# Two query units multiplied side by side, value pages and key stores placed earlier, and work regrouped at three joins of a decoder layer

## The chip, the cores and the metric

The kernel runs on one NeuronCore of one Trainium2 chip. The metric is the time of one execution on the device in microseconds (us). TensorE (PE) multiplies, VectorE (DVE) and ScalarE (ACT) work elementwise, GpSimd (POOL) does a little elementwise work and issues transfers, and SyncE (SP) issues most transfers. Sixteen DMA engines move the data.

## What is computed

One layer of a decoder in fp32 for 256 prompt tokens and 8 sampled tokens (T = 264 columns): a mixer with eight gated delta-net heads and eight block-attention heads, cross attention, and a gated feed-forward, each followed by a layer norm of residual plus result.

```python
def gated_delta_chunked(q, k, v, beta, g): ...   # 8 heads, chunks of 64
def moba_attend(q, kb, vb, kmean, q_pos, rel_bias):
    gate = jnp.einsum('bqhd,bhnd->bqhn', qf, kmean)
    top_s, top_i = lax.top_k(gate, K)            # 3 blocks of 256 cached tokens per sample and head
    kg = kb[bi, hi, idx]; vg = vb[bi, hi, idx]
    ...
    p = jax.nn.softmax(s.reshape(B, Q, H, -1), axis=-1).reshape(s.shape)
    return jnp.einsum('bqhtk,bqhtkd->bqhd', p, vg)

def post_norm(x, sub, g, b):
    return layer_norm(ALPHA * x + sub, g, b)
...
xp = post_norm(xp, mix_p, ln_g[l, 0], ln_b[l, 0])
xp = post_norm(xp, cross_attend(xp, mkp, mvp, x_wq[l], x_wo[l]), ln_g[l, 1], ln_b[l, 1])
xp = post_norm(xp, swiglu(xp, ffn_w1[l], ffn_w2[l]), ln_g[l, 2], ln_b[l, 2])
```

## The kernel before

The work is a sequence of *units*. A unit is one weight tile of 2048 inputs by 128 outputs (1 MB in fp32). Its product with the 264 columns keeps fp32 precision by a split: ACT rounds the tile to its upper part `wh` (L498, `upper`), DVE makes the rest `wl` (L503, `lower`), and PE adds three products for each of the 16 slices of the contraction, `wh*xh` (L519), `wh*xl` (L520) and `wl*xh` (L521), 48 matmuls in all, into one of two banks of `psum_g`. `raw`, `wh` and `wl` have two slots, used in turn by even and odd units. SP loads a tile with `load_unit` (L493) once its slot has been read (`raw_used`). Counting semaphores tie the stages: `raw_full`, `hi_done`, `raw_used`, `mm_done`, `psum_free`. All orders are written out by hand, engine by engine.

The stages, in units: `q` (8, the queries of block attention), `a` (32, the projections of the delta-net heads and the keys of block attention, with 128 pages of cached keys scored in between, L2122), `b` (16, units 32 to 47 of a joint count `u`: eight value units, then eight gates "z"), `out` (16), `wk`, `xq`, `wv`, `xo` (4 each, cross attention), and the feed-forward.

*Start.* SP loads the input x in quarters, each followed by a quarter of unit 0's tile (L615, L616), then unit 1, then 1.1 MB of constants and tables, then unit 2. ACT and DVE split x and the quarters (L865, L867, L1299, L1302). PE multiplies unit 0, then the small products for the gates (`ab`, L2073), then unit 1, a product that turns them (`abt`, L2089 to L2091), units 2, 3 and 4, and the products of the running sums (`cum`, L2097 to L2100). Between the copies of units 2 and 3 ACT computes a sigmoid and a logarithm, with two table loads (L885, L887), and only behind them the upper part of unit 4.

*Value pages.* For each sample and head six pages of cached values (64 KB each, 512 bytes per row) are needed, chosen at run time. They come in 16 groups of four heads. Two heads of a group are loaded by SP and two by GpSimd (`values`, L596 for the page numbers, L604 for twelve loads each). There is room for three groups: group g waits until group g - 3 was used. PE uses a group in 24 products (`page_values`, L2254). `groups_at(u, end)` says which: group 0 after unit 35, group 1 in the middle of unit 36, group 2 behind it, and so on, so that group 15 is used in the middle of unit 43.

GpSimd's own list there is: store a state, clear `zp` (L798), the decay product `tg` of head pair 3 (`decays(3)`, L775), which PE reads in unit 35, the value pages, the store of the last state (L785), and later the store of all keys and values `kv` (L817). SP's list behind its last value group is: four sample states (L671), unit 45, the other four states once GpSimd's last state store has landed (`s_out`), unit 46, rows of the result to a scratch (L706), unit 47.

*Join to the output product.* ACT and DVE split four groups of the mixer's result in the order 2, 3, 0, 1 (L1074, L1102 and L1707); ahead of group 0 DVE gates the last head and the samples (L1577, L1704). ACT then loads a table (L1136) and makes the upper part of unit 1 of `out`.

*Layer norms.* DVE centres and scales groups of `xf` (L1744, L1750), ACT applies gain and offset (L1124) and, in the first norm, the upper part (L1131), DVE the lower (L1758). The first norm has groups of 2, 2, 4, 4 and 4 slices, the last one of 4, 4, 4, 2 and 2. The first norm runs beside the four `wk` units; PE needs its last group for the last quarter of unit 0 of `xq`, and unit 1 of `xq` is split by ACT and DVE behind that group.

## Time and profile before

| what | value |
| --- | --- |
| median of 3 executions | 1602.91 us (1602.39 to 1605.07) |
| the profiled execution's own time | 1602.35 us |
| its span, first to last instruction | 1600.4 us |
| PE busy | 1540.7 us (96%) |
| DVE, ACT, POOL busy | 932.9, 644.2, 182.7 us |
| moved | 365.17 MB, mean 228 GB/s |

The profiled execution is 0.56 us below the median, and 1.95 us of it lie outside its span. PE is busy nearly all the time, so a time is won only where PE stands still or runs at the lower clock, and the profile has to be read at those places.

### The profile page before, as it was taken

The numbers are of one execution on the slowest core, as the hardware profiler recorded it, in microseconds if no ns is written. First come the engines' busy times: TensorE is split into PE (matmuls) and PEld (weight loads), VectorE is DVE, ScalarE is ACT, GpSimd is POOL, SyncE is SP. The second block draws the span as 40 slices with busy tenths as digits, with TensorE's granted clock in tenths as the row PEclk, the third lists the DMA queues.
The fourth block names the chain that finished last, engine by engine and source line by source line (L and its number), as shares of the span: only waits on it lengthen the run. The fifth ranks groups of instructions, "written<-read, shape, count | busy, mean of one in ns | idle before, by whom it ended". The sixth has DMA issues, their size and how long they took to land.

```text
span 1600.4 us, 36185 instructions
## 1 busy us (share of the span) xinstructions
PE 1540.7 (96%) x14680; PEld 1495.3 (93%) x14680; DVE 932.9 (58%) x1130; ACT 644.2 (40%) x752; POOL 182.7 (11%) x286
## 2 busy tenths in 40 slices
PE   7999999999998879999999999999999999999996
PEld 6999999999898779997899999999999999999995
DVE  4445645557753345774487666666666644445566
ACT  5344333343523443464454333544333333333344
POOL 0000202021577510001000000000011000000000
PEclk9999999999999999999999999999999999999998
DMA  8698878886788977455645545555677655555453
GB/s 308 218 338 338 314 282 331 290 319 219 222 250 259 288 281 309 172 184 200 244 163 183 172 171 183 185 180 187 241 261 255 214 185 183 184 183 174 165 179 113
DMA packets 104339, 365.17 MB, mean 228 GB/s; under 512 B 14385, under 2 KB 48378, under 8 KB 77210
## 3 DMA queue, kind: packets, MB, share of 16 engines
q1 hardware_dynamic: 89682, 322.66, 58.0%
q0 software_dynamic: 12752, 39.73, 7.2%
q10 hardware_dynamic: 1792, 1.20, 0.4%
q8 instruction: 79, 1.29, 0.3%
q14 instruction: 34, 0.28, 0.1%
HBM read 353.27 MB, written 10.47 MB: 227 GB/s over the span
## 4 chain that ended last, share of the span: by engine, by line
PE 76%; issue 8%; ACT 5%; DVE 5%; DMA 4%; SPq 2%; POOLq 1%; POOL 1%; ACTq 0%; DVEq 0%
PE psum_g L519 21%; PE psum_g L520 21%; PE psum_g L521 21%; PE M L2122 3%; PE M L2137 3%; DVE wl L503 2%; ACT wh L498 2%; DMA raw<-w_in_t 1%; PE M L519 1%; PE psum_g L2431 1%; PE M L520 1%; PE M L521 1%; DMA sraw<-cache_k_t 1%; SPq L630 1%; ACT xf L1124 1%
## 5 line engine op out<-in xcount | busy, mean ns | idle before, releaser
L519 PE MATMUL psum_g<-xh,wh 128*128 128x264 f32 (+1 forms) x2414 | 709.0, 294 | 24.0 <-DVE wl L503 11.9
L520 PE MATMUL psum_g<-xl,wh 128*128 128x264 f32 (+1 forms) x2414 | 688.8, 285 | 0.0
L521 PE MATMUL psum_g<-xh,wl 128*128 128x264 f32 (+1 forms) x2414 | 687.9, 285 | 0.0
L503 DVE TENSOR_TENSOR wl<-raw,wh 128x2048 fp32r<-128x2048 f32 (+1 forms) x223 | 502.6, 2254 | 310.6 <-ACT wh L498 310.1
L498 ACT CAST wh<-raw 128x2048 fp32r<-128x2048 f32 (+1 forms) x223 | 418.2, 1875 | 248.9 <-PE psum_g L521 204.4
L519 PEld LDWEIGHTS psum_g<-xh,wh 128*128 128x128 f32 x2414 | 458.6, 190 | 40.3 <-issue 23.1
L520 PEld LDWEIGHTS psum_g<-xl,wh 128*128 128x128 f32 x2414 | 458.8, 190 | 3.1 <-issue 2.9
L521 PEld LDWEIGHTS psum_g<-xh,wl 128*128 128x128 f32 x2414 | 457.0, 189 | 0.0
L519 PE MATMUL psum_g<-gh,wh 128*128 128x264 f32 x704 | 200.4, 285 | 0.2 <-DVE wl L503 0.2
L521 PE MATMUL psum_g<-gh,wl 128*128 128x264 f32 x704 | 199.4, 283 | 0.0
L520 PE MATMUL psum_g<-gl,wh 128*128 128x264 f32 x704 | 199.4, 283 | 0.0
L519 PEld LDWEIGHTS psum_g<-gh,wh 128*128 128x128 f32 x704 | 132.5, 188 | 0.6 <-DVE wl L503 0.4
L520 PEld LDWEIGHTS psum_g<-gl,wh 128*128 128x128 f32 x704 | 132.7, 188 | 0.0
L521 PEld LDWEIGHTS psum_g<-gh,wl 128*128 128x128 f32 x704 | 132.0, 187 | 0.0
L2122 PE MATMUL M<-kring,pj 128*32 128x128 f32 x1536 | 61.9, 274 | 0.9 <-DMA sraw<-cache_k_t 0.9
L2137 PE MATMUL M<-chain 128*128 128x128 f32 x448 | 60.4, 276 | 0.1
L2122 PEld LDWEIGHTS M<-kring,pj 128*32 128x32 f32 x1536 | 53.9, 110 | 6.5 <-issue 4.2
L847 POOL DMA_DIRECT2D out_dn_sample<-state x8 | 7.2, 904 | 445.8 <-DVE state L2019 445.8
L604 POOL DMA_DIRECT2D pj<-cache_v x102 | 55.0, 539 | 14.7 <-issue 9.8
L2137 PEld LDWEIGHTS M<-chain 128*128 128x128 f32 x448 | 55.0, 191 | 1.6 <-issue 1.2
L1260 ACT ACTIVATE sg<-psum_g 128x264 f32<-128x264 f32 x28 | 11.0, 392 | 111.1 <-PE psum_g L521 111.1
L1110 ACT ACTIVATE xt<-xf 128x264 f32<-128x264 f32 x32 | 13.6, 425 | 99.8 <-DVE xf L1803 56.0
(431 smaller groups left out, 1698.6 us busy)
## 6 DMA issues: line engine op xcount, KB each, us to landing
raw<-w_t SPq DMA_DIRECT2D x88, 1024.0 KB, 4.9
raw<-w_in_t SPq DMA_DIRECT2D x55, 1024.0 KB, 7.8
kring<-cache_k_t SPq DMA_DIRECT2D x96, 512.0 KB, 4.6
sraw<-cache_k_t SPq DMA_DIRECT2D x32, 512.0 KB, 6.1
raw<-w_out_t SPq DMA_DIRECT2D x16, 1024.0 KB, 5.1
raw<-w2a_t SPq DMA_DIRECT2D x16, 1024.0 KB, 4.8
raw<-w2b_t SPq DMA_DIRECT2D x16, 1024.0 KB, 4.9
raw<-w2c_t SPq DMA_DIRECT2D x16, 768.0 KB, 4.2
```

The costliest lines, as they stand in the source:

```text
L498: nc.scalar.copy(wh[:, u % 2, 0:nk], raw[:, u % 2, 0:nk]).then_inc(hi_done, 1)
L503: eng.tensor_tensor(wl[:, u % 2, 0:nk], raw[:, u % 2, 0:nk], wh[:, u % 2, 0:nk].bitcast(F32), ALU.subtract).then_inc(raw_used, 1)
L519: nc.tensor.matmul(out, hi_w, x_hi(k), start=(k == order[0]), stop=False)
L520: nc.tensor.matmul(out, hi_w, x_lo(k), start=False, stop=False)
L521: last = nc.tensor.matmul(out, lo_w, x_hi(k), start=False, stop=(k == order[-1]))
L604: eng.dma_start(v_pages[s][:, t], a["cache_v"][0, ds(pages[6 * n_ + t], 1), :, h].rearrange("a t d -> t (a d)"))\
L630: _, pages = nc.values_load_multi_w_load_instructions(page_turns[j:j + 1], engines={mybir.EngineType.SP}, min_val=0, max_val=k_pages.shape ...
L1110: nc.scalar.activation(xt[:, u % 2], m, ACT.Square).then_inc(sq_made, 1)
L1124: ins = nc.scalar.activation(xf[:, k], xf[:, k], ACT.Identity, bias=ln_gb[:, 1, i, k:k + 1], scale=ln_gb[:, 0, i, k:k + 1])
L2122: last = nc.tensor.matmul(M[rows:rows + 32, pg // 4, (pg % 4) * P:(pg % 4 + 1) * P], qz[:, b + 4 * (p % 2), h], k_slot(m)[:, h * P:(h + 1) ...
L2137: last = nc.tensor.matmul(out(w), lhs(w), rhs(w), start=True, stop=True)
L2431: last = nc.tensor.matmul(psum_g[:, t], m[:, 4 * u + k, t * P:(t + 1) * P], w_at(w, k), start=(u == 0 and k == 0 and w is wh and m is mem_ ...
```

## The change

The diff, cut to its core:

```diff
         def groups_at(u, end):
 
-            group = 2 * (u - KEY_UNITS - 3) + end - 1
-            return (group,) if 0 <= group < 16 else ()
+            first = 2 * (u - KEY_UNITS - 3)
+            groups = {(0, 1): (0,), (2, 0): (1,), (2, 1): (2, 3)}.get((first, end), (first + end,) if first > 2 else ())
+            return tuple(g for g in groups if g < 16)
...
-        E_OUT = 16 * 2
+        E_OUT = 16 * 3
...
+            parts = [slice(per * g, per * (g + 1)) for g in range(PARTS)]
+            first, second, third = (w_tile(a["w_in_t"], KTAIL + u) for u in range(3))
+            for g, part in enumerate(parts):
+                end = g == PARTS - 1
                 sp.dma_start(x_in[:, part], a["x_t"][:, part]).then_inc(d_x[g], 16)
-                sp.dma_start(raw[:, 0, part], w_tile(a["w_in_t"], KTAIL)[:, part])\
-                  .then_inc(d_w[g] if g < PARTS - 1 else raw_full[0], 16)
-            load_unit(sp, turn, 1, w_tile(a["w_in_t"], KTAIL + 1))
-            sp.dma_start(C[:], a["constants"]).then_inc(d_const, 16)
+                sp.dma_start(raw[:, 0, part], first[:, part]).then_inc(raw_full[0] if end else d_w[g], 16)
+                sp.dma_start(raw[:, 1, part], second[:, part]).then_inc(raw_full[1] if end else d_v[g], 16)
+            for g, part in enumerate(parts):
+                wait(sp, s_dve, f"lw{g}")
+                sp.dma_start(raw[:, 0, part], third[:, part]).then_inc(raw_full[0] if g == PARTS - 1 else d_y[g], 16)
+            sp.dma_start(C[:, 0:P], a["constants"][:, 0:P]).then_inc(d_eye, 16)
+            load_unit(sp, turn, 3, w_tile(a["w_in_t"], KTAIL + 3))
+            sp.dma_start(C[:, P:], a["constants"][:, P:]).then_inc(d_const, 16)
...
-            for u in range(2, 4 * n):
+            for u in range(4, 4 * n):
                 load_unit(sp, turn + u // 4, u % 4, w_tile(a["w_in_t"], KTAIL + u))
-                if 3 <= u < 7:
-                    half = u - 3
-                    load_pages(half // 2, range(2 * (half % 2), 2 * (half % 2) + 2))
+                half = u - 4
+                load_pages(half // 2, range(2 * (half % 2), 2 * (half % 2) + 2))
...
             nc.gpsimd.memset(zp_flat, 0.0).then_inc(e_pool.sem, 1)
-            decays(3)
+            pool.wait_ge(psum_free, 4 * turn + KEY_UNITS + 2)
+            pool.dma_start(o["kv"][:, 0:8], kv[:, 0:8]).then_inc(e_out, 16)
             pool.wait_ge(pid_back, 16)
             values(0)
+            decays(3)
             values(1)
...
-            for name, tile in (("kv", kv), ("edge", edge)):
-                pool.dma_start(o[name], tile[:]).then_inc(e_out, 16)
+            pool.dma_start(o["kv"][:, 8:16], kv[:, 8:16]).then_inc(e_out, 16)
+            pool.dma_start(o["edge"], edge[:]).then_inc(e_out, 16)
...
+                act.wait_ge(d_v[g] if g < PARTS - 1 else raw_full[1], 16)
+                nc.scalar.copy(wh[:, 1, part], raw[:, 1, part]).then_inc(s_act.sem, 1)
+            act.sem_inc(hi_done, 2)
...
-
-            upper_next(act, turn, 0)
+                scaled(u)
+
             unit_done(act, turn, 0)
-            nc.scalar.mul(qb[:, 0], psum_g[:, 0, 0:T], SCALE).then_inc(psum_free, 1)
+            for g in range(2):
+                act.wait_ge(d_y[g], 16)
+            nc.scalar.copy(wh[:, 0, 0:2 * per], raw[:, 0, 0:2 * per]).then_inc(s_act.sem, 1)
+            act.wait_ge(d_y[2], 16)
+            act.wait_ge(raw_full[0], 32)
+            nc.scalar.copy(wh[:, 0, 2 * per:], raw[:, 0, 2 * per:]).then_inc(hi_done, 1)
+            scaled(0)
+            scaled(1)
             wait(act, s_pe, "ab")
             nc.scalar.copy(abt, M[:, 0, 0:T]).then_inc(s_act.sem, 1)
-            queries(1)
             queries(2)
+            upper_next(act, turn, 3)
...
-            queries(3)
+            scaled(3)
...
-            act.preload_act_table_set("natural_log_exp_and_others")
             for i in range(n):
                 for u in range(4):
                     upper_next(act, turn + i, u)
+                    if i == 0 and u == 0:
+                        act.preload_act_table_set("natural_log_exp_and_others")
...
                        after={1: lambda: (memory_keys(1), upper_next(act, turn, 2)),
-                              2: lambda: (memory_keys(2), upper_next(act, turn, 3))})
-            memory_keys(3)
+                              2: lambda: (memory_keys(2), upper_next(act, turn, 3)),
+                              3: lambda: (memory_keys(3), upper_next(act, STAGES["xq"][0], 0))})
             turn, n = STAGES["xq"]
             for u in range(4):
-                upper_next(act, turn, u)
+                if u:
+                    upper_next(act, turn, u)
...
+                wait(dve, s_act, f"hv{g}")
+                nc.vector.tensor_tensor(wl[:, 1, part], raw[:, 1, part], wh[:, 1, part].bitcast(F32),
+                                        ALU.subtract).then_inc(s_dve.sem, 1)
+            wait(dve, s_dve, f"lv{PARTS - 1}")
+            dve.sem_inc(raw_used, 2)
             turn, n = STAGES["q"]
-            lower_next(dve, turn, 0)
-            settle(dve)
+            wait(dve, s_act, "h2")
+            nc.vector.tensor_tensor(wl[:, 0, 0:2 * per], raw[:, 0, 0:2 * per], wh[:, 0, 0:2 * per].bitcast(F32),
+                                    ALU.subtract).then_inc(s_dve.sem, 1)
+            dve.wait_ge(hi_done, 3)
+            nc.vector.tensor_tensor(wl[:, 0, 2 * per:], raw[:, 0, 2 * per:], wh[:, 0, 2 * per:].bitcast(F32),
+                                    ALU.subtract).then_inc(raw_used, 1)
+            dve.wait_ge(d_eye, 16)
...
-                if g == 0:
+                if g == 3:
                     gated(H - 1)
...
+                    for g in (4, 5):
                         centre(g)
                         scale(g)
-                    low(2)
-                low(3)
-                low(4)
+                    low(3)
+                    at("n5")
+                    low(4)
+                    low(5)
...
-            def quarter(k):
-                if k % per == 0:
-                    wait(pe, s_dve, f"lw{k // per}")
-
-            products(pe, psum_g[:, 0, 0:T], 0, lambda w, s, k: w[:, s, k], XH, XL, KC, before=quarter, done=mm_done)
+            for g in range(PARTS):
+                for s in range(2):
+                    wait(pe, s_dve, f"l{'wv'[s]}{g}")
+                    for k in range(per * g, per * (g + 1)):
+                        out, end = psum_g[:, s, 0:T], k == KC - 1
+                        nc.tensor.matmul(out, wh[:, s, k], xh[:, k], start=(k == 0), stop=False)
+                        nc.tensor.matmul(out, wh[:, s, k], xl[:, k], start=False, stop=False)
+                        last = nc.tensor.matmul(out, wl[:, s, k], xh[:, k], start=False, stop=end)
+                        if end:
+                            last.then_inc(mm_done, 1)
             pe.wait_ge(d_ab, 16)
             for i in range(4):
                 last = ab_products(i)
             last.then_inc(s_pe.sem, 1)
-            unit(pe, turn, 1, XH, XL)
+            wait(pe, s_dve, "l2")
+            pe.wait_ge(psum_free, 3)
+            products(pe, psum_g[:, 0, 0:T], 0, lambda w, s, k: w[:, s, k], XH, XL, KC,
+                     before=lambda k: pe.wait_ge(raw_used, 5) if k == 2 * per else None, done=mm_done)
...
-            unit(pe, turn, 2, XH, XL)
```

- **Start.** Units 0 and 1 are loaded, split and multiplied quarter by quarter side by side; unit 2's tile is loaded in quarters as the quarters of unit 0 become free; the constants come as a small first part (the identity, with a semaphore of its own) and a rest behind unit 3. PE runs the `ab` product behind both units and `abt` behind unit 2. The upper part of unit 4 stands ahead of ACT's table loads.
- **Value pages.** GpSimd issues its part of group 0 ahead of `decays(3)`. Groups 2 and 3 are both used behind unit 36, and each later group half a unit before its former place, so that group 15 is used behind unit 42. `kv` is stored in two halves: the keys ahead of GpSimd's value pages once unit 31 has been copied, the values at the old place (`E_OUT` counts three transfers).
- **Join to the output product.** DVE does the last gate and the samples between groups 2 and 3, and ACT loads its table behind the upper part of unit 1.
- **Layer norms.** Both norms now have groups of 2, 2, 4, 4, 2 and 2 slices; in the first, the split of unit 1 of `xq` stands ahead of the last two groups' lower parts (`n5`), on ACT ahead of the last two groups.

On ACT near the start, before (the cast `wh<-raw` of 128x2048 is a whole unit's upper part, `qb<-psum_g` the copy of a finished unit; row 28 is the upper part of unit 4):

```order
18 L498 CAST wh<-raw 128x2048
19 L875 ACTIVATE qb<-psum_g 128x264
20 L498 CAST wh<-raw 128x2048
21 L875 ACTIVATE qb<-psum_g 128x264
22 L885 ACT_TABLE_LOAD
23 L885 ACTIVATE sigm<-kv 128x24
24 L887 ACT_TABLE_LOAD
25 L888 ACTIVATE kv<-kv 128x24
26 L890 ACTIVATE kv<-kv 128x24
27 L892 ACTIVATE kv<-kv 128x8
28 L498 CAST wh<-raw 128x2048
29 L875 ACTIVATE qb<-psum_g 128x264
```

And in the changed program:

```order
22 L898 COPY kv<-M 128x264
23 L497 CAST wh<-raw 128x2048
24 L882 ACTIVATE qb<-psum_g 128x264
25 L497 CAST wh<-raw 128x2048
26 L902 ACT_TABLE_LOAD
27 L902 ACTIVATE sigm<-kv 128x24
28 L904 ACT_TABLE_LOAD
29 L905 ACTIVATE kv<-kv 128x24
30 L907 ACTIVATE kv<-kv 128x24
31 L909 ACTIVATE kv<-kv 128x8
32 L882 ACTIVATE qb<-psum_g 128x264
```

The upper part of unit 4 (row 25) now stands ahead of both table loads.

On POOL behind the state store of pair 2, before (`chain<-C,g_hc` is `decays(3)`; the loads from `cache_v` go on to the twelfth):

```order
26 L785 DMA out_dn_prompt<-chain 128x2x128
27 L798 MEMSET kring 128x720
28 L775 TENSOR_TENSOR chain<-C,g_hc 128x512
29 L596 TENSOR_LOAD C
30 L604 ISA
31 L604 DMA pj<-cache_v 128x128
32 L604 ISA
```

And in the changed program, with the place where group 0 ends shown too:

```order
26 L789 DMA out_dn_prompt<-chain 128x2x128
27 L802 MEMSET kring 128x720
28 L804 DMA out_kv<-kv 128x2112
29 L595 TENSOR_LOAD C
30 L603 ISA
31 L603 DMA pj<-cache_v 128x128
...
53 L603 DMA pj<-cache_v 128x128
54 L779 TENSOR_TENSOR chain<-C,g_hc 128x512
55 L595 TENSOR_LOAD C
```

The decay product moved from row 28 to row 54, behind the twelve loads of group 0, and a store of 128x2112 went in ahead of them.

On DVE at the join to the output product, before (`xl<-qb,xh` are groups 2 and 3, `pj<-C` the samples, `xl<-pj,xh` groups 0 and 1, then two clears and the lower part of unit 1):

```order
431 L1577 TENSOR_TENSOR pj<-pj,C 128x256
432 L1707 TENSOR_TENSOR xl<-qb,xh 128x1056 x2
433 L1577 TENSOR_TENSOR pj<-pj,C 128x256
434 L1704 TENSOR_TENSOR pj<-C 128x8x8
435 L1707 TENSOR_TENSOR xl<-pj,xh 128x1056 x2
436 L1725 MEMSET acc 128x264
437 L1726 MEMSET acc 128x264
438 L503 TENSOR_TENSOR wl<-raw,wh 128x2048
```

And in the changed program:

```order
436 L1603 TENSOR_TENSOR pj<-pj,C 128x256
437 L1733 TENSOR_TENSOR xl<-qb,xh 128x1056
438 L1603 TENSOR_TENSOR pj<-pj,C 128x256
439 L1730 TENSOR_TENSOR pj<-C 128x8x8
440 L1733 TENSOR_TENSOR xl<-qb,xh 128x1056
441 L1733 TENSOR_TENSOR xl<-pj,xh 128x1056 x2
442 L1751 MEMSET acc 128x264
443 L1752 MEMSET acc 128x264
444 L502 TENSOR_TENSOR wl<-raw,wh 128x2048
```

The last gate and the samples moved ahead of group 3.

## Rows read from the trace of the kernel before

**Rows 1.** The page: busy time, share of the span, instructions.

```profile
PE 1540.7 (96%) x14680; PEld 1495.3 (93%) x14680; DVE 932.9 (58%) x1130; ACT 644.2 (40%) x752; POOL 182.7 (11%) x286
```

**Rows 2.** Waits of PE: engine, line, waited for: us in total, times, longest.

```profile
PE psum_g L519 <- DVE wl L503: 12.1, 11, 2.8
PE M L2254 <- DMA pj<-cache_v: 9.3, 4, 4.3
```

**Rows 3.** Timeline of the start: start us, duration, engine, line, in brackets idle before.

```profile
8.29 0.56 PE L519 MATMUL psum_g<-xh,wh 128*128 128x264 f32 x1 [8.29 <-DVE wl L1302]
13.58 1.26 DVE L1299 TENSOR_TENSOR xl<-pj,xh 128x1056 fp32r<-128x1056 f32 x1
14.76 0.69 DVE L1302 TENSOR_TENSOR wl<-raw,wh 128x512 fp32r<-128x512 f32 x1
17.15 2.01 PE L2073 MATMUL M<-pj,kv 128*32 128x264 f32 x32
36.65 1.89 ACT L498 CAST wh<-raw 128x2048 fp32r<-128x2048 f32 x1
40.92 0.59 PE L519 MATMUL psum_g<-xh,wh 128*128 128x264 f32 x1 [2.23 <-DVE wl L503]
48.28 0.29 PE L2097 MATMUL M<-gates,C 128*128 128x16 f32 x2
```

**Rows 4.** Timeline, ACT: copies of two finished units with no wait between them.

```profile
62.53 0.39 ACT L875 ACTIVATE qb<-psum_g 128x264 f32<-128x264 f32 x1 [2.96 <-PE psum_g L521]
68.33 0.39 ACT L875 ACTIVATE qb<-psum_g 128x264 f32<-128x264 f32 x1 [3.62 <-PE psum_g L521]
```

**Rows 5.** The chain that ended last: one matmul at the lower, one at the full clock.

```profile
41.51 0.22 PE psum_g L520
45.53 0.12 PE psum_g L519
```

**Rows 6.** Timeline: POOL around its value pages, PE's use of `tg` (L2148).

```profile
411.49 1.04 POOL L775 TENSOR_TENSOR chain<-C,g_hc 128x512 f32<-128x512 f32 x1 [5.78 <-DVE pj L1466]
417.50 1.02 PE L2148 MATMUL M<-chain,C 128*128 128x512 f32 x2
421.54 7.04 POOL L604 DMA_DIRECT2D kring<-cache_v  x12 [0.90 <-issue]
544.91 0.72 POOL L785 DMA_DIRECT2D out_dn_prompt<-chain  x1
```

**Rows 7.** Timeline of SP: the fourth and the last value group, states, unit 46.

```profile
430.55 8.52 SPq L604 DMA_DIRECT2D pj<-cache_v  x12
534.41 7.01 SPq L604 DMA_DIRECT2D pj<-cache_v  x12
551.27 0.92 SPq L671 DMA_DIRECT2D chain<-state_dn  x2
559.25 1.28 SPq L493 DMA_DIRECT2D raw<-w_in_t  x1
```

**Rows 8.** Timeline of PE: groups 14 and 15, and unit 47.

```profile
541.77 0.27 PE L2254 MATMUL M<-kring 128*8 128x128 f32 x1 [4.35 <-DMA pj<-cache_v]
550.20 1.50 PE L2254 MATMUL M<-pj,kring 128*8 128x128 f32 x48 [1.27 <-DMA pj<-cache_v]
582.38 0.39 PE L519 MATMUL psum_g<-xh,wh 128*128 128x264 f32 x1 [2.85 <-DVE wl L503]
```

**Rows 9.** Windows: busy time of each engine, clock, DMA share, GB/s.

```profile
404.00:412.00 8.00, 8.00 (x58) 7.04 (x57) 6.76 (x11) 5.65 (x11) 1.98 (x3) 1.00 0.40 113
412.00:540.00 128.00, 116.39 (x1422) 107.74 (x1420) 63.03 (x120) 46.93 (x91) 99.47 (x185) 1.00 0.90 263
```

**Rows 10.** Timeline of the join to the output product, ACT and PE.

```profile
594.60 1.28 ACT L1136 ACT_TABLE_LOAD   x1
600.18 0.39 PE L519 MATMUL psum_g<-xh,wh 128*128 128x264 f32 x1 [2.05 <-DVE wl L503]
```

**Rows 11.** Timeline of PE: unit 1 of `xq`, beside the first layer norm.

```profile
725.86 0.39 PE L519 MATMUL psum_g<-xh,wh 128*128 128x264 f32 x1 [1.38 <-DVE wl L503]
```

57 lines of the change are left out of this document (23 added, 34 removed).

## The prediction

> **What bounds the kernel now.** I read the page first: PE is busy for 96% of the span [rows 1], so only places where PE stands still or is slowed can give time. The waits of PE say where: 12.1 us in eleven waits for the lower part of a weight tile and 9.3 us in four for value pages [rows 2] (the largest groups of that list). Then the timelines of those places.
>
> *Start.* From PE's first product at 8.29 to the products of the running sums at 48.28 there are 40.0 us [rows 3]. Work in them: five units of 5.80 us each, the distance of two copies of units between which nothing waits [rows 4], so 29.0; the `ab` products 2.0 [rows 3]; the three `abt` products, about 0.6; and some 23 matmuls at the lower clock level (1.2 GHz) ahead of 13.3 us at 0.22 instead of 0.12 us [rows 5], so 2.3. That is 34.0; 6.0 is loss. Its largest piece is unit 4: PE stands for 2.2 us ahead of 40.92, because ACT made that unit's upper part at 36.65, behind two table loads [rows 3], and the first 14 matmuls of unit 4 run at the lower level again, another 1.4. The rest are waits for quarters and for the tiles of units 1 and 2.
>
> *Value pages.* The chain that ended last runs through POOL's page loads from 421 to 544.9, so POOL looks like the bound. But SP issues the other half of the pages, and it stands still nowhere either: its group 3 begins at 430.55, its group 15 ends at 541.42, at 534.41 + 7.01 [rows 7]. POOL ends 3.5 us later, at 544.91 [rows 6]. A reader should see both queues here, since PE needs both halves. PE waits 4.35 us for group 14 and 1.27 for group 15 [rows 8].
>
> *Tail of the mixer.* POOL's last state store lands, SP goes on to the states at 551.27 and to unit 46 at 559.25 [rows 7], and by that tile, the rows of the result and unit 47's tile the wait of 2.85 us ahead of 582.38 comes about [rows 8].
>
> *Joins.* Unit 1 of `out` starts at 600.18 behind 2.05 us of waiting, with a table load of 1.28 us on ACT just ahead of its upper part [rows 10]. Unit 1 of `xq` starts at 725.86, 1.38 us late [rows 11].
>
> **The change part by part.** The sum is made against the profiled execution, 1602.35 us; the median of the runs shown lies 0.56 higher.
>
> *Start, -5.8.* The work of 34.0 us stays. It remains gapless if each step is ready in time. DVE, the slowest feeder, needs 1.26 + 2 x 0.69 = 2.64 us for a quarter of x and of both units [rows 3], and PE works 24 matmuls on it, 2.9 us at full clock: PE is the slower. Loads: 4.1 MB (x and two tiles) instead of 3.1 MB ahead of the last quarter put that quarter's end some 2.5 us later, at about 16; PE reaches it at about 19.3 (8.3, then 23 matmuls slow and 49 fast). Units 0 and 1 end at 22.2, `ab` at 24.2. Unit 2's halves are split from 20.8 (end of unit 0) to 24.3 on DVE, its first half by 23.1, so unit 2 starts at about 24.3 and ends at 30.1. Unit 3 follows `abt`, to 36.7. The upper part of unit 4 begins at about 30.6, its lower part ends at 34.9: 1.8 us ahead of PE. The table loads fall behind that, and nobody waits for them: the gate values are needed at 42.5. So the sums' products come at 8.3 + 34.0 = 42.3, or 42.5 with small gaps, where they were at 48.28. If the cover of unit 4's tile is gone (it is issued behind the constants and eight small transfers, at about 25, and takes 5 to 6 us), each us later than 32.4 is lost one for one. Bounds: -4.5 (a residual gap of 1.3) and -6.5. What comes behind is paced by PE, so the gain holds through stage `a`, and the page numbers, SP's and POOL's first values all move with it; times below are still those of the trace of before.
>
> *POOL's first pages, keys' store.* POOL has nothing to do between the clear at 405 and 411.49 [rows 6]. The keys' store costs it one issue (0.6 us) and 1.1 MB of DMA work, in a stretch with the DMA engines 40% busy [rows 9], so I cost it at nothing; with that cover gone it costs 1.1 MB at 263 GB/s, 4 us of DMA work. Twelve loads take 7.04 us [rows 6], so group 0 goes out from about 407.5 to 414.7, and `tg` is ready at about 415.8; PE wants it at 417.5, in unit 35 [rows 6]. POOL's group 1 then starts at 416.5 instead of 421.5, and every later one 5 us earlier; and of the 4.3 us that its 15 groups from 421.54 on take over 15 x (0.90 + 7.04) [rows 6], some 3 were waits for a room that the earlier use frees. POOL would end at about 536.5 instead of 544.9.
>
> *Pages used earlier.* This takes away 8 us of slack from each group after group 2. SP's part isn't moved: no room kept it waiting (its groups follow one another at 8.5 us, from 430.55 to 541.42 for 13 groups [rows 7]). Its last group still ends at 541.4 and lands some 3.5 us later, at 545. With SP's ends as the clock, PE waits a little at groups 10, 11, 14 and 15 (1.8, 2.8, 3.1 and 2.0 us), finishes group 15 at 546.4 and, with all of unit 43 still to come (7.3 us at full clock), ends that unit at 553.7, where it was at 554.8: -1.1. Behind it, SP goes from its four states straight to the other four at about 549.9 instead of 551.27 [rows 7], -1.4; and its eight slow state issues, and unit 46's tile, meet a DMA load without POOL's last group (0.8 MB) and, for the tile, nothing of the keys: worth 0 to 3 us. I take **-2.5** for the tail at unit 47. Bounds: 0 (SP's pace falls as POOL's pages crowd it) and -8.4 (POOL alone was the bound, and SP's pace rises with the load gone).
>
> The Trainium skill bears on this: the page "DMA: Bandwidth & Descriptors", section "Issuing engines are not separate DMA queues", says that transfers started on several engines end up on the same 16 DMA engines and interleave, so that issuing on another engine saves only sequencer time. By that rule POOL's earlier issues would give nothing in a stretch where the engines are full. By the row, they are 90% busy from 412 to 540 and 40% ahead of it [rows 9]: group 0 goes into the empty part, the rest has little room.
>
> *Join to `out`, -3.0.* Samples and last gate are done 0.7 us earlier, so groups 0 and 1 are split 0.7 to 1.1 earlier; group 3's lower part comes 0.8 later, for a wait of 0.3. ACT's upper part of unit 1 moves by 0.9 + 1.28 [rows 10]; DVE follows it at once. Unit 1 starts at about 598.1 instead of 600.18: -2.1. From 600 to 604 PE ran at the lower level for most of the time, about 1.7 us lost; the lower level came behind that wait of 2.05 us and smaller ones ahead of it. With a wait of 0.3 and one of 1.0 left I count half of that, 0.9. Bounds: -1.0 (the transfers for cross attention that begin there give part back) and -3.8.
>
> *First norm, -1.8.* Unit 1 of `xq` is split at 716.9 to 721.9 instead of 721.57 to 725.8, and its start is set by group 5's lower part, for which PE ends unit 0 at about 724.0 instead of 724.5, starting unit 1 at 724.0, not 725.86 [rows 11]. Bounds -1.0, -2.1. *Last norm, -0.2.* ACT starts its 16 instructions earlier, since the first group is half as wide, but DVE's centring and scaling of the same 16 slices sets the middle, and the last group ends hardly earlier. Bounds 0, -0.5.
>
> Sum: -5.8 - 2.5 - 3.0 - 1.8 - 0.2 = **-13.3**; 1602.35 - 13.3 = 1589.05, against the median **1589.6**.
>
> **Rivals.**
> 1. *POOL was the whole bound.* For it: the chain of the profile runs through POOL. Against it: SP ends only 3.5 us ahead. The value stretch and tail give 7 to 8 instead of 2.5, about 1584.5.
> 2. *The value stretch gives nothing.* SP's queue stays the bound and loses as much pace to POOL's earlier pages as the end gains; PE's waits only move. Tail 0, join 2: 1593.
> 3. *The start doesn't become gapless.* Unit 2's or unit 4's tile is late by 3 us and PE falls to the lower level once more, 1.4: the start gives 1.5, about 1594.
> 4. *Slower.* SP loses pace in the value stretch: its groups now take 8.5 us, where twelve loads take 7.01 at one time and 8.52 at another [rows 7], so a good part is pushing against busy DMA engines. PE now asks half a unit earlier, so nothing covers a lag. From 13.3 / 13, about 1.0 us more for each of 13 groups, the whole gain is gone; at 1.3 more the kernel takes 1606. The DMA engines' 90% [rows 9] leave 10%, about 0.9 us of a group, and no bytes are added, so this is unlikely.
>
> **How the numbers follow.** Chances: the forecast (1587 to 1592) 0.50, POOL whole bound 0.20, value stretch nothing 0.20, start not gapless 0.06, slower 0.03, an outcome between -3 and +3 us 0.01. The time is that of the likeliest, 1589.6, its own range 1587 to 1592. The range of 0.8 takes in the first three with their bounds: 1583 to 1595.5. About 0.2% (3.2 us) is what a measurement here tells from no change; faster by more than that 0.95, within it 0.02, slower 0.03.
>
> **What would show it.** Start: the sums' products at 42 to 43, no wait over 0.5 us ahead of them but the first, no second slow stretch. Value pages: POOL's last page load ends 8 us earlier against unit 31's end, SP's last one as before; PE's waits for pages at groups 9 to 15, none of 4 us. Tail: unit 46's tile issued 2 to 4 us earlier. Join: table load behind the upper part, full clock in unit 1. Norm: `xq` unit 1 without a wait over 0.3. I am wrong if SP's own loads become quicker once POOL's are out of the way (then the tail gives more), if `tg` is late in unit 35, or if the slow clock level comes back in some other gap.

## The result, and the profile after

The changed kernel takes 1612.62 us (median of 9 runs, 1609.32 to 1616.96), the kernel before 1604.53 (median of 9, 1602.39 to 1609.93). The ratio is 1.0055, with a 95% interval of 1.004 to 1.007: slower by 8 to 9 us, where 13.3 us less were forecast (1589.6 us). The profiled execution took 1612.62 us with a span of 1610.8, against 1602.35 and 1600.4.

PE's busy time has not grown much; the line of the page that answers to [rows 1] has 2.8 us more of it, while the span is 10.4 us longer:

```profile
PE 1543.5 (96%) x14680; PEld 1496.0 (93%) x14680; DVE 934.3 (58%) x1139; ACT 645.6 (40%) x757; POOL 184.0 (11%) x287
```

The waits of PE, summed (engine, line, waited for: us in total, times, longest), are to be read beside [rows 2]:

```profile
PE M L2284 <- DVE kring L1582: 19.1, 7, 4.2
...
PE psum_g L518 <- DVE wl L502: 8.6, 10, 2.2
```

The reader should see that the largest group is new. L2284 is the product with value pages. Before, it waited 9.3 us for pages in four waits [rows 2], and once more for a page of the other buffer, in a row of the same view that the prediction leaves out:

```profile
PE M L2254 <- DMA kring<-cache_v: 2.8, 1, 2.8
```

That makes 12.1 us in five waits. Now it waits 19.1 us in seven, and for DVE. DVE's line 1582 is the small copy that spreads one sample's probabilities into `zp`, from which PE loads its weights; it was never named in the prediction. Six of the seven stand at the first group of a sample (groups 4, 6, 8, 10, 12, 14): 4.19, 4.20, 3.60, 2.07, 1.83 and 2.46 us. Three of them in the timeline of PE; the columns are start, duration, engine, line, idle before and releaser:

```profile
458.23 2.75 PE L2284 MATMUL M<-kring 128*8 128x128 f32 x48 [4.19 <-DVE kring L1582]
...
480.19 2.75 PE L2284 MATMUL M<-pj,kring 128*8 128x128 f32 x48 [4.20 <-DVE kring L1582]
...
519.95 1.50 PE L2284 MATMUL M<-kring 128*8 128x128 f32 x48 [2.07 <-DVE kring L1582]
```

DVE at the first two of these places:

```profile
455.44 0.42 DVE L1598 COPY qb<-M 128x256 f32<-128x256 f32 x1
455.77 2.28 DVE L502 TENSOR_TENSOR wl<-raw,wh 128x2048 fp32r<-128x2048 f32 x1
457.97 0.20 DVE L1582 COPY kring<-pj 128x48 f32<-128x48 f32 x1
...
477.73 2.28 DVE L502 TENSOR_TENSOR wl<-raw,wh 128x2048 fp32r<-128x2048 f32 x1
479.93 0.20 DVE L1582 COPY kring<-pj 128x48 f32<-128x48 f32 x1
```

The copy ends at 458.17 and at 480.13; PE goes on at 458.23 and 480.19, and so it is at all six, 0.05 to 0.06 us behind. It takes 0.2 us, but stands behind the lower part of the next tile (2.28 us), which stands behind the head's result (0.42 us) and a step of the delta net that waited 2.65 us for PE ahead of 453.63.

The start did what was said. The products of the running sums (L2127, in the kernel before at 48.28 [rows 3]) come at 43.16, 5.1 us earlier, and there is no wait over 0.15 us on PE between its first product at 8.61 and there. The next row is the first wait behind it:

```profile
43.16 0.29 PE L2127 MATMUL M<-gates,C 128*128 128x16 f32 x2
...
64.56 0.39 PE L518 MATMUL psum_g<-xh,wh 128*128 128x264 f32 x1 [1.39 <-DVE wl L502]
```

How far the changed kernel is ahead (-) or behind (+), by the starts of the same units in both profiled executions, and what each stretch cost:

| place | before | after | difference | gained or lost in the stretch |
|---|---|---|---|---|
| products of the sums | 48.28 | 43.16 | -5.1 | -5.1 |
| unit 35 of the mixer | 415.94 | 416.46 | +0.5 | +5.6 |
| unit 47 of the mixer | 582.38 | 596.76 | +14.4 | +13.9 |
| unit 5 of `out` | 626.01 | 638.54 | +12.5 | -1.9 |
| first product with `mem_k`, behind `xq` | 744.00 | 754.60 | +10.6 | -1.9 |
| end of the span | 1600.4 | 1610.8 | +10.4 | -0.2 |

So the start, the join and the norms gave about what was forecast or less, and two stretches took it back: 5.6 us in that of the keys' pages, 13.9 us in that of the value pages. The second can be split. From unit 35 to unit 47 PE does the same work in both kernels:

```profile
415.94:582.38 166.44, 147.89 (x1842) 137.37 (x1842) 76.24 (x148) 56.90 (x106) 104.50 (x193) 0.99 0.92 276
```

```profile
416.46:596.76 180.30, 153.62 (x1842) 140.66 (x1843) 77.08 (x148) 56.81 (x106) 100.78 (x186) 0.95 0.84 250
```

The first is the kernel before, the second the changed one (stretch, length, busy time of PE, its weight loads, DVE, ACT and POOL, clock, DMA share, GB/s). PE stands for 26.7 us instead of 18.6, which is 8.1 us of the 13.9, and its 1842 products take 5.7 us more at a granted clock of 0.95 instead of 0.99.

### The profile page after: what moved, and what is told of

Read it like the earlier page. It is cut to its first block, busy times and chain, and to the rows that moved or that the text cites. A ratio compares the mean times of both kernels' runs of the same rounds, so it can differ in the third digit from the quotient of the medians.

```text
span 1610.8 us, 36205 instructions
## 1 busy us (share of the span) xinstructions
PE 1543.5 (96%) x14680; PEld 1496.0 (93%) x14680; DVE 934.3 (58%) x1139; ACT 645.6 (40%) x757; POOL 184.0 (11%) x287
## 4 chain that ended last, share of the span: by engine, by line
PE 81%; DVE 7%; ACT 4%; DMA 3%; SPq 3%; issue 2%; ACTq 0%; DVEq 0%
PE psum_g L518 22%; PE psum_g L519 21%; PE psum_g L520 21%; PE M L2167 4%; PE M L2152 3%; DVE wl L502 3%; SPq L635 2%; ACT wh L497 2%; PE M L2284 1%; DMA raw<-w_out_t 1%; PE M L518 1%; PE psum_g L2461 1%; PE M L519 1%; PE M L520 1%; DMA raw<-w_in_t 1%
## 5 line engine op out<-in xcount | busy, mean ns | idle before, releaser
L518 PE MATMUL psum_g<-xh,wh 128*128 128x264 f32 (+1 forms) x2382 | 697.9, 293 | 10.6 <-DVE wl L502 8.4
L519 PE MATMUL psum_g<-xl,wh 128*128 128x264 f32 (+1 forms) x2382 | 678.0, 285 | 0.0
L520 PE MATMUL psum_g<-xh,wl 128*128 128x264 f32 (+1 forms) x2382 | 677.1, 284 | 0.0
L518 PEld LDWEIGHTS psum_g<-xh,wh 128*128 128x128 f32 x2382 | 450.9, 189 | 26.8 <-issue 16.1
L519 PEld LDWEIGHTS psum_g<-xl,wh 128*128 128x128 f32 x2382 | 451.1, 189 | 3.1 <-issue 2.9
L520 PEld LDWEIGHTS psum_g<-xh,wl 128*128 128x128 f32 x2382 | 449.2, 189 | 0.0
```

The lines of the kernel that those rows point to most:

```text
L518: nc.tensor.matmul(out, hi_w, x_hi(k), start=(k == order[0]), stop=False)
L519: nc.tensor.matmul(out, hi_w, x_lo(k), start=False, stop=False)
L520: last = nc.tensor.matmul(out, lo_w, x_hi(k), start=False, stop=(k == order[-1]))
```

## The experiments

The theory: in the value stretch PE waits for DVE's copy, not for pages, because the first group of a sample is now used in the middle of a unit and the copy is made behind the lower part. The rivals: the pages are late themselves (SP's or GpSimd's queue), and the copy only comes at the same moment. For the start: the lead is lost in SP's reads of page numbers, or to the DMA engines' rate, or by chance. All ratios are to the kernel before, with their 95% intervals; it was timed again beside the runs (medians of 1604.46 to 1606.03 over 17 to 23 executions), and a ratio can differ by 0.001 from the quotient of two medians. "Stretch" is the time from the start of unit 35 to that of unit 47 in the profiled execution (166.4 us before, 180.3 in the changed kernel).

**The copy early.**

```
@@ DVE, at the head of each unit of the mixer
                 if 0 <= j - 1 < H:
                     scores_norm(j - 1)
+                if 2 <= u - KEY_UNITS - 3 < NSAMP:
+                    spread(u - KEY_UNITS - 3)
                 step(0)
...
                 lower(dve, turn, u + 1)
-                elif 0 < u - KEY_UNITS - 3 < NSAMP:
+                elif u == KEY_UNITS + 4:
                     spread(u - KEY_UNITS - 3)
```

> The changed kernel, with DVE's copy of a sample's probabilities for samples 2 to 7 put right behind the heads' scaling, ahead of the lower part of the next tile and of the head's result. In the changed kernel six value products (458.23, 480.19, 502.38, 519.95, 536.78, 553.18) each begin 0.05 us behind the end of that copy, after waits of 4.19, 4.20, 3.60, 2.07, 1.83 and 2.46 us, 18.4 in all. Theory (the copy is what the pages' earlier use waits for): these six waits go, the copy stands 5 to 8 us earlier, and the value stretch falls back to what the pages allow; unit 47 then starts about 13 us earlier against unit 35 than in the changed kernel, and the kernel takes about 1599, 1597 to 1602. Rival (the pages themselves are late, and the copy only comes at the same moment): the copies move, the products keep their times within 1 us, and the kernel takes 1610 to 1613.

Measured: 1596.22 us, ratio 0.9949 (0.9935 to 0.9963), stretch 164.1 us. One copy of 0.2 us for each sample, put elsewhere, is worth 1.0055 - 0.9949, a little over 1% of the time, 16 to 17 us. The time is 3 us under the theory's 1599, just outside its range. The longest waits of PE for value pages now, and then, on DVE, the copy that had ended at 480.13:

```profile
450.96 0.73 PE L2286 MATMUL M<-kring 128*8 128x128 f32 x20 [0.89 <-DMA kring<-cache_v]
...
501.67 1.24 PE L2286 MATMUL M<-kring 128*8 128x128 f32 x18 [4.58 <-DMA kring<-cache_v]
...
532.90 0.27 PE L2286 MATMUL M<-kring 128*8 128x128 f32 x1 [1.14 <-DMA pj<-cache_v]
```

```profile
462.99 0.22 DVE L1582 COPY kring<-pj 128x48 f32<-128x48 f32 x1
```

The reader should see that the releasers are pages again (`kring<-cache_v`, `pj<-cache_v`), 7.6 us in four waits, and that the copy for group 6 is done at 463.21 while PE comes to that group at 467.07. The theory's waits are gone, all six. The rival is refuted: the products moved with the copy, so most of the 18.4 us were not the pages'.

**The old places of use**, with everything else of the change:

```
         def groups_at(u, end):
-            first = 2 * (u - KEY_UNITS - 3)
-            groups = {(0, 1): (0,), (2, 0): (1,), (2, 1): (2, 3)}.get((first, end), (first + end,) if first > 2 else ())
-            return tuple(g for g in groups if g < 16)
+            group = 2 * (u - KEY_UNITS - 3) + end - 1
+            return (group,) if 0 <= group < 16 else ()
```

> The changed kernel with the pages used where the kernel before uses them; GpSimd's first pages ahead of the decay product, the stored keys in two halves, the start, the join and the norms stay changed. Theory (only the earlier use puts the value products in front of DVE's copy): the six waits behind the copy go, as in the kernel before, and the stretch from unit 35 to unit 47 takes what it took before, 166.4 us and not 180.3; with the 1.9 of the join and the 1.7 of the norm the kernel takes about 1600, 1597 to 1602. If GpSimd's earlier pages are worth what the prediction gave the tail, it is 2.5 less. Rival (GpSimd's earlier pages crowd the Sync queue's, and that makes the waits): the stretch stays over 175 us and the kernel above 1608.

Measured: 1597.59 us, ratio 0.9947 (0.9934 to 0.9959), stretch 165.5 us. The second way to put the copy ahead of its user gives the same time. So, with GpSimd's first pages early in both kernels, using pages half a unit earlier is worth nothing that these runs can tell from no change.

**The value pages' part alone, and with the copy early.** The kernel before, with `groups_at` of the change, `values(0)` ahead of `decays(3)` and the keys stored in two halves; the second of the two also with the edit of the copy above. GpSimd's part of the edit:

```
+            pool.wait_ge(psum_free, 4 * turn + KEY_UNITS + 2)
+            pool.dma_start(o["kv"][:, 0:8], kv[:, 0:8]).then_inc(e_out, 16)
-            decays(3)
             pool.wait_ge(pid_back, 16)
             values(0)
+            decays(3)
             values(1)
```

> The kernel before with the change of the value pages alone (pages used half a unit earlier, GpSimd's first pages ahead of the decay product, stored keys in two halves), DVE's copy where it was. Theory (the waits behind DVE's copy cost 12 to 13 us between units 35 and 47, and nothing of the start or the joins takes part in it): 1616 to 1619 against 1604.5 to 1606, ratio 1.006 to 1.009. Rival (it was the meeting of the earlier start with the pages that cost so much): ratio below 1.003.

Measured: 1618.45 us, ratio 1.0073 (1.0057 to 1.009), stretch 182.8 us, with the same six waits of 4.20, 4.20, 3.60, 2.07, 1.82 and 2.47 us.

> As the run with the value pages alone, and DVE's copy for samples 2 to 7 ahead of the lower part. Theory (with the copy in time, the pages' earlier use is worth what the prediction gave the tail, 2.5 us, less the 0.9 that the decay product costs beside DVE): ratio about 0.9985, 0.998 to 0.9995. Rival (the start's lead is what makes the earlier use pay): ratio 1.000 or above.

Measured: 1603.66 us, ratio 0.9984 (0.9972 to 0.9996), stretch 164.4 us. The loss of the value stretch is in this part and needs nothing of the others; with the copy in time, the part gains about 2.6 us (0.6 to 4.5 by the interval), near what the prediction gave the tail.

**GpSimd's decay product first again**, on the kernel with the copy early:

```
+            decays(3)
             pool.wait_ge(psum_free, 4 * turn + KEY_UNITS + 2)
             pool.dma_start(o["kv"][:, 0:8], kv[:, 0:8]).then_inc(e_out, 16)
             pool.wait_ge(pid_back, 16)
             values(0)
-            decays(3)
```

> The changed kernel with DVE's copy early, and GpSimd's last decay product ahead of its first value pages again, as in the kernel before. With the pages first, the decay product takes 2.65 us instead of 1.04 and lies beside DVE's multiply for the keys (1.26 instead of 0.42 us); PE's wait ahead of the own-key products is 1.4 instead of 0.5 us. Theory (the two engines hold each other up when they work on memory at the same time, and GpSimd's pages are not the bound since the Sync queue ends 1.2 us behind it): the 0.9 us come back, GpSimd's pages are 2 us later at first, and the kernel takes 0 to 1 us less than with the early copy alone, ratio 0.9945 to 0.995. Rival (the prediction's: the pages 5 us earlier are worth something): the kernel takes 1 to 3 us more, ratio 0.9955 to 0.997.

Measured: 1603.21 us, ratio 0.9992 (0.9983 to 1.0001), stretch 171.7 us. That is beyond both expectations: the order of these two is worth 0.9992 - 0.9949, 7 us, where pages are used early. GpSimd's timeline in this kernel, and then in the one with the pages first:

```profile
412.68 1.03 POOL L779 TENSOR_TENSOR chain<-C,g_hc 128x512 f32<-128x512 f32 x1 [5.79 <-DVE pj L1492]
413.66 0.60 POOL L805 DMA_DIRECT2D out_kv<-kv  x1
414.66 1.73 POOL L603 DMA_DIRECT2D pj<-cache_v  x3 [0.39 <-issue]
```

```profile
402.24 0.58 POOL L804 DMA_DIRECT2D out_kv<-kv  x1
403.25 2.33 POOL L603 DMA_DIRECT2D pj<-cache_v  x4 [0.44 <-issue]
...
410.68 2.71 POOL L779 TENSOR_TENSOR chain<-C,g_hc 128x512 f32<-128x512 f32 x1
```

The product waits 5.79 us for DVE, and the pages stand behind it. Their first load goes out 2.5 us ahead of unit 35 (414.66 against 417.14) instead of 9.3 us (403.25 against 412.55): 6.8 us later. Its second group goes out 5.8 us behind the start of unit 35 instead of 0.8 (422.97 and 413.35), 5.0 us later. In this kernel PE waits 5.98 us for group 3, and 3.10 for group 15; SP's groups 3 to 15 run from 432.84 to 540.78, 8.3 us each as with the pages first (428.99 to 536.35), so SP's queue has no part in it. The product itself took 1.03 us here.

**The start alone, and the joins and norms alone**, on the kernel before:

> The kernel before with the changed start alone (units 0 and 1 side by side, unit 2's tile in halves, constants split, the keys' pages asked for one unit later). Theory of the trace: the products of the running sums come 5 us earlier (43.2 and not 48.3), stage a gives all of it back in waits for a tile and for the keys' pages, unit 35 starts where it did within 1.5 us, and the kernel takes 1603 to 1606, no change. Rival (the prediction's, the gain holds and what the changed kernel lost in stage a is chance of one execution): 1597 to 1600.

Measured: 1602.82 us, ratio 0.9983 (0.9973 to 0.9994): 2.7 us, between the two expectations. The sums' products come at 42.23, 6.0 us earlier; unit 35 starts at 411.44, 4.5 us earlier, so that stage `a` kept most of the lead here, against the theory; the stretch then takes 168.8 us instead of 166.4, with 4.93 us of waiting for group 14's pages and 1.75 for the states, and unit 47 is 2.2 us early.

> The kernel before with the two joins and the norms of the change alone (table load behind the upper part of unit 1 of out, the last gate ahead of group 3; six parts of a norm, unit 1 of xq split within it). The prediction's theory: -3.0 at the join, -1.8 at the first norm, -0.2 at the last one, 1599 to 1600.5. The trace of the changed kernel says -1.9 and -1.7 and nothing at the end: about 1601 against 1604.5 to 1606 of the kernel before, a ratio of 0.998. Rival (both joins' time comes back in waits for tiles behind them): ratio 0.9995 to 1.001.

Measured: 1600.97 us, ratio 0.9979 (0.9969 to 0.999), -3.4 us, about what the trace of the changed kernel said (1.9 and 1.9). Together the three parts alone make 0.9983 + 0.9979 + 1.0073 - 2 = 1.0035, against 1.0055 (1.004 to 1.007) of all at once; with the copy early 0.9983 + 0.9979 + 0.9984 - 2 = 0.9946, against 0.9949. The sums of three carry an uncertainty of about 0.002, so the account closes within the intervals.

**The page numbers of the keys.** SP reads the numbers of a sample's pages from memory into registers, behind the issue of a weight tile. First, both reads ahead of the tile's issue, in the changed kernel (the mixer's place; the queries' units are changed in the same way):

```
-                load_unit(sp, turn, u + 1, mixer_tile(u + 1))
-                for j in bursts_at(u):
-                    if j >= 2:
-                        load_pages(j)
+                bursts = [j for j in bursts_at(u) if j >= 2]
+                pages = [page_numbers(j) for j in bursts]
+                load_unit(sp, turn, u + 1, mixer_tile(u + 1))
+                for j, numbers in zip(bursts, pages):
+                    load_pages(j, numbers)
```

> The changed kernel, with the Sync engine reading the page numbers of the keys ahead of a weight tile's issue and no longer behind it; the tile and the pages follow in the same order. In the changed kernel the two reads behind a tile's issue take 1.6 to 6.1 us together, and in the longest of them the DMA engines run at 0.53 of their time (115 to 120 us). Theory (the start's gain is lost because the Sync engine stands in those reads while tile and pages could be under way): the waits at 64.56 (1.39), 125.91 (1.27), 135.87 (2.00) and 331.06 (1.38) go for the most part, unit 35 starts 3 to 6 us earlier, and the kernel takes 1607 to 1610. Rival (the DMA engines, at 0.78 to 0.88 of their time from 45 to 340 us, are the bound there, and an earlier start only waits longer): unit 35 starts where it does, within 1 us, and the kernel takes 1611 to 1614.

Measured: 1612.01 us, ratio 1.0044 (1.0031 to 1.0057), no change from 1.0055, and unit 35 starts 1.1 us earlier, not 3 to 6. But the rival isn't borne out as it stood either: the waits for key pages at 126 and 136 us are gone. What was gained there was lost ahead of it, in the queries' units, where PE waits 0.63 and 1.78 us for tiles at 51.73 and 59.58. So the two places were then treated apart, on the kernel with the copy early: in the queries' units the numbers are read once for two halves; then also ahead of the tile in the mixer.

```
                 half = u - 4
-                load_pages(half // 2, range(2 * (half % 2), 2 * (half % 2) + 2))
+                if half % 2 == 0:
+                    pages = page_numbers(half // 2)
+                load_pages(half // 2, pages, range(2 * (half % 2), 2 * (half % 2) + 2))
```

> The changed kernel with DVE's copy early, as in the run with the early copy alone, and with the page numbers of the keys read once for each two halves of a sample's pages in the units of the queries, not once for each half. The tile of unit 8 is issued at 53.65 in the changed kernel, behind a read of 4.65 us that only repeats an earlier one, and PE waits 1.4 us for that tile ahead of 64.56. Theory (that read is what is late): the wait goes, the lead over the kernel before stays at 4.5 to 6 us until 85 us, and the kernel takes 1 to 2.5 us less than with the early copy alone, a ratio of about 0.994 to 0.9935. Rival (the tile waits for the DMA engines' work in any case): PE waits 1.2 to 1.5 us there again, same time as with the early copy alone, 0.9949.

Measured: 1594.25 us, ratio 0.994 (0.9925 to 0.9954). SP's read at 46.3 us in the changed kernel (duration min, median, max in ns, first and last start), SP's issues behind it, and the same issues where the numbers are read once:

```profile
L635 SPq TENSOR_LOAD <-page_turns_ptr x1: 4647/4647/4647, 46.3 to 46.3; - x1
```

```profile
45.81 0.43 SPq L492 DMA_DIRECT2D raw<-w_in_t  x1
52.74 0.86 SPq L640 DMA_DIRECT2D sraw<-cache_k_t  x2
53.65 11.21 SPq L492 DMA_DIRECT2D raw<-w_in_t  x3
```

```profile
43.75 0.43 SPq L492 DMA_DIRECT2D raw<-w_in_t  x1
44.78 0.86 SPq L642 DMA_DIRECT2D sraw<-cache_k_t  x2
49.45 7.36 SPq L492 DMA_DIRECT2D raw<-w_in_t  x2
```

Unit 8's tile goes out at 49.45, not 53.65. The wait ahead of that unit (1.39 us in the changed kernel) is gone, and the lead at 85 us, by the start of the same lower part on DVE, is 5.5 us, against 3.5 in the changed kernel and 4.3 in the run with the copy early, on which this edit is made.

> As the run with the numbers read once, and in the mixer stage they are read ahead of a weight tile's issue. With the reads ahead of the tile in both stages the waits for key pages at 102 to 136 and at 331 us went (0.5 instead of up to 4.7 us), but 2.4 us were lost in the units of the queries, where PE takes 5.8 us for a unit and the reads held the tiles up. Theory (reads that the Sync engine stands in cost the lead wherever the tile or the pages are the next to be late): with the start's reads once and the mixer's ahead, the lead at 350 us is 5 to 6 us, and the kernel takes 2 to 3.5 us less than with the early copy alone, a ratio of about 0.993. Rival (the DMA engines' rate bounds 60 to 340 us): the lead falls to 1 to 3 us by 350 us whatever the reads do, ratio 0.995.

Measured: 1593.39 us, ratio 0.9935 (0.9922 to 0.9947). The lead at 350 us is 5.2 us, and the largest wait for key pages 0.92 us, at 235. The step from 0.9949 through 0.994 to 0.9935 goes the way of the theory, but each step is smaller than the intervals; what is shown by the traces is that the waits moved.

> As the run with the start alone, and the page numbers of the keys read once for two halves. Theory (the repeated read holds unit 8's tile up and costs 1.4 us of waiting, and 1.3 more of the lead by 65 us): the lead is 5 us until stage a's key pages, and the ratio 0.997, against 0.9983 of the start alone. Rival (the value stretch takes the rest back, since pages and not PE set its end): unit 47 starts 2.2 us earlier as with the start alone, ratio 0.998 to 0.9985.

Measured: 1603.18 us, ratio 0.9985 (0.9973 to 0.9996), no better than the start alone: the rival's number. The lead is 3.5 us at unit 35 and 1.7 us at unit 47. With the pages used at the old places and GpSimd late, the value stretch takes a lead back. Beside the other parts the start gives about the same: without it they make 0.9984 + 0.9979 - 1 = 0.9963, and with it 0.9949 was measured, 2.2 us less; with it and the numbers once and early 0.9935, 4.5 us less.

**The decay product between the two heads of GpSimd's group 0**, on the kernel with the numbers once and early:

```
             for n_, h in enumerate(heads):
+                if n_:
+                    between()
...
-            values(0)
-            decays(3)
+            values(0, between=lambda: decays(3))
```

> As the run with the numbers read once and early, and with GpSimd's last decay product between its two heads of group 0, not behind them. Behind them the product (1.05 us) falls beside DVE's lower part of unit 35's tile, which takes 3.62 instead of 2.29 us, and PE waits 2.32 instead of 1.00 us ahead of unit 35. DVE stands idle for 2.2 us ahead of that lower part, and GpSimd has issued group 0's first six pages by then. Theory (the two engines hold each other up): product and lower part take 1.05 and 2.29 us, PE's wait is 1.0, and the kernel takes about 1.3 us less than in the run with the numbers once and early, ratio about 0.9925. Rival (the 3.62 us have another cause, the wait stays at 2.3 us): ratio 0.9935.

Measured: 1593.27 us, ratio 0.9918 (0.9904 to 0.9933), 0.8% under the kernel before. GpSimd's product and DVE's lower part without this edit (numbers once and early), and then with it:

```profile
408.81 1.05 POOL L784 TENSOR_TENSOR chain<-C,g_hc 128x512 f32<-128x512 f32 x1
...
408.41 3.62 DVE L502 TENSOR_TENSOR wl<-raw,wh 128x2048 fp32r<-128x2048 f32 x1 [2.19 <-ACT wh L497]
```

```profile
408.41 1.03 POOL L786 TENSOR_TENSOR chain<-C,g_hc 128x512 f32<-128x512 f32 x1 [1.04 <-DVE pj L1498]
...
410.52 2.29 DVE L502 TENSOR_TENSOR wl<-raw,wh 128x2048 fp32r<-128x2048 f32 x1 [2.20 <-ACT wh L497]
```

The lower part takes 2.29 us again, and PE's wait ahead of unit 35 is 1.00 instead of 2.32 us. Whether the 1.3 us show in the time is open: the intervals of the two runs overlap, their medians differ by 0.1 us, and behind unit 35 the stretch of this profiled execution is 1.8 us longer, with waits for pages of 0.93 and 3.09 us at 442.84 and 453.74 that the other doesn't have.

All runs, in the order of their times:

| kernel | us | ratio | unit 35 | unit 47 | stretch |
|---|---|---|---|---|---|
| decay between the heads (numbers once and early, copy early) | 1593.27 | 0.9918 | 412.87 | 577.35 | 164.5 |
| numbers once and early, copy early | 1593.39 | 0.9935 | 412.08 | 574.78 | 162.7 |
| numbers once, copy early | 1594.25 | 0.994 | 412.19 | 575.18 | 163.0 |
| copy early | 1596.22 | 0.9949 | 412.55 | 576.66 | 164.1 |
| old places of use | 1597.59 | 0.9947 | 416.15 | 581.62 | 165.5 |
| joins and norms alone | 1600.97 | 0.9979 | 414.99 | 580.38 | 165.4 |
| start alone | 1602.82 | 0.9983 | 411.44 | 580.23 | 168.8 |
| start alone, numbers once | 1603.18 | 0.9985 | 412.44 | 580.71 | 168.3 |
| copy early, decay product first | 1603.21 | 0.9992 | 417.14 | 588.87 | 171.7 |
| pages' part alone, copy early | 1603.66 | 0.9984 | 420.58 | 584.99 | 164.4 |
| numbers early, copy late | 1612.01 | 1.0044 | 415.40 | 595.65 | 180.3 |
| pages' part alone, copy late | 1618.45 | 1.0073 | 415.98 | 598.75 | 182.8 |

## Why the prediction was wrong, point by point

*Start, forecast -5.8.* Right in mechanism and nearly in size up to the sums' products (-5.1). Wrong was the sentence behind it: "What comes behind is paced by PE, so the gain holds through stage `a`". First, only unit 4's tile was followed; unit 8's tile is the one that came late. It was issued at 53.65, behind a read of page numbers of 4.65 us, since the pages' loads now stand one unit later while PE is five us earlier. That cost 1.4 us of waiting, and 1.9 of the lead by 67 us. Second, in stage `a` SP reads numbers for 1.9 to 6.2 us for each four pages, and whether the pages are there when PE wants them is near the edge in the kernels that read behind the tile: at about 136 us PE waited 0.50 us before and 2.00 in the changed kernel, and 1.27 more at 125.91. The place where the changed kernel lost most is this:

```profile
125.91 0.86 PE L2152 MATMUL M<-kring,pj 128*32 128x128 f32 x23 [1.27 <-DMA kring<-cache_k_t]
...
135.87 0.30 PE L2152 MATMUL M<-kring,pj 128*32 128x128 f32 x2 [2.00 <-DMA sraw<-cache_k_t]
...
331.06 0.71 PE L2152 MATMUL M<-kring,pj 128*32 128x128 f32 x17 [1.38 <-DMA kring<-cache_k_t]
```

How much it loses there is partly chance. Five profiled executions with the same code up to unit 32 started unit 35 with a lead of 4.5, 3.4, -0.2, -0.5 and -1.2 us; three with the old start, of leads of 1.0, 0.0 and -4.6 (the last two have 1.4 us of the decay product in it, the last one also a wait of 3.04 us at 139.56). What the start is worth over 12 runs, its run alone shows: 2.7 us (1.0 to 4.3 by the interval), not 5.8. The three executions with the numbers read ahead of the tile had no wait of 0.15 us or more between 100 and 200 us; why the wait at 136 us differs so much from run to run of the others stays open.

*GpSimd's first pages, forecast 5 us earlier at no cost.* The mechanism was right: with the copy early, GpSimd's second group starts 0.8 us behind unit 35 instead of 5.6, 4.8 us earlier. Its last load, forecast 8 us earlier, ended 6.4 us earlier (122.6 us behind unit 35 instead of 129.0), with the old places of use as well, so the 3 us of waits for rooms that the earlier use should free are not shown; in the changed kernel it ended 0.6 us later. Mis-sized was "`tg` is ready at about 415.8": the product started at 414.66 but took 2.65 us, not 1.04 [rows 6], and DVE's multiply beside it 1.26 us, not 0.42:

```profile
414.66 2.65 POOL L779 TENSOR_TENSOR chain<-C,g_hc 128x512 f32<-128x512 f32 x1
...
414.12 2.29 DVE L502 TENSOR_TENSOR wl<-raw,wh 128x2048 fp32r<-128x2048 f32 x1 [2.20 <-ACT wh L497]
416.33 1.26 DVE L1415 SCALAR_TENSOR_TENSOR pj<-kv 128x256 f32<-128x256 f32 x1
```

DVE's lower part of 414.12 runs to 416.41, and the product lies beside most of it; the multiply from 416.33 lies beside the rest of the product, which ended at 417.31. That delays the own-key products by 0.9 us (a wait of 1.43 us, where it was 0.50, and 0.51 with the decay product first). The Trainium skill, page "SBUF — State Buffer", section "SBUF: two separate sides", says that DVE and GpSimd share a port pair that one of them holds for a whole instruction while the other stands. In the changed kernel the trace agrees, with 2.65 for 1.04 and 1.26 for 0.42 us. That the one which starts first keeps it, as the Trainium skill has it, does not fit by the recorded starts: DVE's lower part began first in eight kept traces, and which of the two was slowed differs. Where GpSimd's product began 0.45 to 0.54 us behind it (changed kernel, copy early, old places, numbers early), the product took 2.65 to 2.74 us; where it began 0.40 to 0.44 us behind (numbers once, numbers once and early, both runs of the pages' part), the product took 1.05 us and the lower part 3.62 to 3.65 instead of 2.29, with 1.3 us more of waiting ahead of unit 35.

*Pages used earlier, the step that failed.* "This takes away 8 us of slack from each group after group 2", the text said, and then followed two of the three things that a value product waits for: GpSimd's half of the pages and SP's. The third is DVE's copy, and its slack was nowhere counted. The trace of before had it, in three rows that the prediction doesn't use (PE's groups 3 and 4, and DVE's copy for group 4):

```profile
451.27 1.50 PE L2254 MATMUL M<-pj,kring 128*8 128x128 f32 x48
...
459.58 1.50 PE L2254 MATMUL M<-kring 128*8 128x128 f32 x48
```

```profile
455.28 0.20 DVE L1556 COPY kring<-pj 128x48 f32<-128x48 f32 x1
```

The copy ends at 455.48, 4.1 us ahead of group 4. The change puts group 4 where group 3 was, at 451.27: 4.2 us ahead of its copy. The wait in the changed kernel is 4.19. The same subtraction, made in the trace of before for all six copies, gives:

| group | its copy ends | new place, that of the group ahead | copy late by | wait measured |
|---|---|---|---|---|
| 4 | 455.48 | 451.27 | 4.21 | 4.19 |
| 6 | 471.62 | 467.41 | 4.21 | 4.20 |
| 8 | 487.14 | 483.53 | 3.61 | 3.60 |
| 10 | 501.76 | 499.98 | 1.78 | 2.07 |
| 12 | 518.99 | 517.16 | 1.83 | 1.83 |
| 14 | 533.52 | 531.04 | 2.48 | 2.46 |

Only group 10 is off by more than 0.02 us, and there group 9 had itself waited 2.55 us for its pages. The loss could be read off before the change was made. So six waits of 18.4 us took the place of 12.1 us for pages, and behind the waits PE fell to its lower level (1.2 GHz): 48 matmuls behind the first two take 2.75 us instead of 1.50. The windows of the stretch, to be read beside [rows 9], and in the run with the copy early:

```profile
412.00:540.00 128.00, 108.20 (x1288) 98.97 (x1287) 57.77 (x106) 36.34 (x73) 96.24 (x176) 0.95 0.88 256
458.00:520.00 62.00, 51.91 (x593) 46.95 (x597) 23.21 (x46) 12.54 (x27) 43.34 (x82) 0.89 0.81 235
```

```profile
412.00:540.00 128.00, 116.06 (x1445) 106.81 (x1445) 62.16 (x120) 42.70 (x84) 99.64 (x183) 0.99 0.95 272
```

The DMA engines were less busy than before (0.88 against 0.90 here, 0.84 against 0.92 from unit 35 to unit 47), for the queues waited for rooms that PE freed late: GpSimd stood 3.03 us ahead of 483.64 and 4.58 ahead of 505.74, both for L2284. With the copy early they are at 0.95 and the clock at 0.99.

*Tail, forecast -2.5.* Near in size, once the copy is out of the way: the stretch takes 164.1 us with the copy early and 164.4 with that part alone, where it took 166.4, and unit 46's tile goes out 2.6 us earlier against unit 35, as forecast. In part that is luck. The old places of use give the same time (0.9947), so what is gained comes from GpSimd's first pages: start and joins alone make 0.9983 + 0.9979 - 1 = 0.9962. The earlier use without GpSimd's earlier pages costs time even with the copy early: 0.9992 against 0.9962, about 5 us. The first rival (GpSimd the whole bound, -7 to -8) is not borne out by these times. The Trainium skill, page "DMA: Bandwidth & Descriptors", section "Issuing engines are not separate DMA queues", had been weighed there: transfers of several engines share the same DMA engines, so that only the time to issue them is saved. The runs don't speak against it, but in this kernel that time decided: GpSimd takes 7.0 us to issue twelve loads, and to begin 6.8 us earlier, in a stretch with room, was worth 7 us where the pages are used early. At the old places it is worth about 2.4 us (0.9962 against 0.9947), which is within the intervals of the three runs.

*Fourth rival, slower (1606).* The sign was right, and the mechanism was not. SP doesn't lose pace to pages asked for earlier: with the copy early its groups 3 to 15 take 107.4 us, 8.3 each, where they took 8.5 [rows 7]. A chance of 0.03 for a loss was too small where 13 uses are moved and not all that they wait for is followed.

*Join, forecast -3.0.* The 2.1 us at unit 1 of `out` came (2.2), and so did the clock: 1.00 where it was 0.57 in the kernel before. What the sum didn't have is that the tiles behind it are then late: PE waits 1.21 and 1.27 us where it waited 0.82, with the DMA engines at 0.93 to 1.04 of their time. The join is worth 1.9. On ACT the upper part now stands ahead of the table load [rows 10]; then two of the tile waits, the window of the kernel before and those of the changed one:

```profile
607.85 1.91 ACT L497 CAST wh<-raw 128x2048 fp32r<-128x2048 f32 x1
609.78 1.28 ACT L1157 ACT_TABLE_LOAD   x1
...
625.40 0.39 PE L518 MATMUL psum_g<-xh,wh 128*128 128x264 f32 x1 [1.21 <-DVE wl L502]
...
638.54 0.38 PE L518 MATMUL psum_g<-xh,wh 128*128 128x264 f32 x1 [1.27 <-DVE wl L502]
```

```profile
600.00:604.00 4.00, 3.81 (x19) 3.82 (x19) 2.15 (x4) 2.22 (x2) 2.97 (x6) 0.57 0.96 401
```

```profile
612.00:616.00 4.00, 3.68 (x30) 3.68 (x31) 2.14 (x4) 2.23 (x2) 3.85 (x8) 1.00 0.93 387
...
620.00:624.00 4.00, 4.00 (x35) 3.98 (x33) 0.95 (x1) 1.91 (x1) 0.00 (x0) 1.00 1.04 426
```

*First norm, forecast -1.8; last norm, -0.2.* The first measured -1.9, but not where it was forecast. The wait ahead of unit 1 of `xq` was to go and is still 1.10 us of 1.38, at 735.00, for a part of x (`xl`) and not for the tile; what went is a wait inside unit 0, 1.65 us at 722.75 before and 0.24 at 732.18 now. The size is luck. The last norm's -0.2 can't be told from chance: from the first product with `mem_k` to the end the kept traces take 856.1 to 859.0 us.

## What to carry to other kernels

Before a consumer is moved earlier, list every semaphore that it waits on, and for each the place of its producer in its own engine's order, what stands ahead of it there and what that in turn waits for. The old trace then gives the price: the producer's end less the user's new place, which came to within 0.02 us for five of six waits here. A wait that never shows in a profile has slack, not zero cost: the cheapest producer (0.2 us, on an engine that is busy for 58% of the span) cost 14 to 17 us when its user was moved past it. And a gain at the start of a long program is only worth what the stages behind it let through: test each part alone before the parts are added up.

## What the runs showed of the hardware

SP's read of a page table from memory into registers took 0.8 to 5.6 us, and with the second read behind it 1.9 to 6.2 us (34 pairs in the changed kernel, 154 us in all, in which SP issues nothing), against 0.74 to 0.93 us for SP's reads of the value page numbers, which it takes from the tile `C`. It isn't the tile's issue ahead of them that makes the pairs long: put ahead of that issue they took 1.4 to 6.7 us. And an operation of GpSimd that takes 1.04 us alone took 2.65 to 2.74 us beside DVE's work, or made DVE's take 1.33 to 1.36 us longer; put into 2 us in which DVE stood idle, it took 1.03 us, and DVE's lower part 2.29.
